# Residual product, norm and split of a two-block transformer: from separate stages to one stage each

## The reference, cut to what matters

```python
# block 1
x = x + g_a * (concat(y_m, y_a) @ w_out)                       # "mix"
x = x + g_f * conv_glu(modulate(rmsnorm(x, norm_ffn), sh_f, sc_f), w_up, conv, w_down)   # "down1"
x = rmsnorm(x, final_norm)                                     # "final1"
# block 2
h = rmsnorm_2(x, attn_norm_g)                                  # "norm2"
x = x + merge(mixers(h)) @ w_out_2                             # "out2"
h = rmsnorm_2(x, ffn_norm_g)
x = x + (silu(a) * b) @ w_down_2                               # "down2"; a, b = split(h @ w_up_2)
out = rmsnorm_2(x, final_norm_g)                               # "final2"
```

## Time and profile before

| | |
|---|---|
| median of 3 runs | 4328.44 us (4320.7 to 4330.6) |
| the profiled execution | 4323.73 us, span 4321.8 us |
| PE busy | 3732.9 us, 86% of the span |
| DVE busy | 1472.4 us, 34% |
| ACT busy | 1071.1 us, 25% |
| POOL busy | 812.3 us, 19% |
| mean granted TensorE clock | 0.924 |

### The profile page before, as it was taken

The page is one execution under the profiler, slowest core; times in us unless marked ns, Lnnn a source line. Parts: engine busy times, 40 slices in busy tenths (PEclk is TensorE's granted clock), DMA queues, the critical chain, the costliest instruction groups (busy, mean ns, idle before and its releaser), DMA issues. The chain is left out here.

```text
span 4321.8 us, 48005 instructions
## 1 busy us (share of the span) xinstructions
PE 3732.9 (86%) x17607; PEld 2966.1 (69%) x17607; DVE 1472.4 (34%) x2062; ACT 1071.1 (25%) x1871; POOL 812.3 (19%) x648
## 2 busy tenths in 40 slices
PE   5689799975999979946999895699998869999896
PEld 3467677863888867634888674377776648888674
DVE  5245352533333333342224443033343320000334
ACT  3423421223111122320222351033332220000222
POOL 3111132200333300012222453011111013332000
PEclk7799999987999989978999996799999979999998
DMA  7510111032111122112111014222222321111321
GB/s 233 191 26 23 40 32 58 1 110 75 49 49 49 39 102 88 63 68 47 44 49 60 29 28 106 56 91 92 90 91 99 104 68 49 49 49 29 131 91 69
DMA packets 282857, 304.16 MB, mean 70 GB/s; under 512 B 28810, under 2 KB 234794, under 8 KB 281046
## 3 DMA queue, kind: packets, MB, share of 16 engines
q1 hardware_dynamic: 279496, 275.57, 20.9%
q10 hardware_dynamic: 2846, 26.03, 1.9%
q0 software_dynamic: 384, 0.81, 0.1%
HBM read 261.03 MB, written 40.67 MB: 70 GB/s over the span
## 5 line engine op out<-in xcount | busy, mean ns | idle before, releaser
L170 PE MATMUL ps<-h_hi,w_hi 128*128 128x512 f32 x1408 | 549.7, 390 | 83.5 <-POOLq L200 83.5
L170 PE MATMUL ps<-h_lo,w_hi 128*128 128x512 f32 x1408 | 549.2, 390 | 0.0
L170 PE MATMUL ps<-h_hi,w_lo 128*128 128x512 f32 x1408 | 549.0, 390 | 0.0
L170 PEld LDWEIGHTS ps<-h_hi,w_hi 128*128 128x128 f32 x1408 | 265.4, 188 | 140.0 <-POOLq L200 85.1
L2187 PE MATMUL ps<-xn_hi,w_hi 128*128 128x512 f32 x608 | 250.1, 411 | 87.8 <-POOL w_lo L2152 49.7
L1600 PE MATMUL ps<-src_hi,w_hi 128*128 128x512 f32 x960 | 254.0, 404 | 81.8 <-ACTq L1555 75.7
L170 PEld LDWEIGHTS ps<-h_lo,w_hi 128*128 128x128 f32 x1408 | 265.4, 188 | 55.3
L170 PEld LDWEIGHTS ps<-h_hi,w_lo 128*128 128x128 f32 x1408 | 265.2, 188 | 55.1
L1571 DVE TENSOR_TENSOR w_lo<-w_raw,w_hi 128x1024 fp32r<-128x1024 f32 x120 | 147.0, 1225 | 443.6 <-ACTq L1555 443.5
L1600 PEld LDWEIGHTS ps<-src_hi,w_hi 128*128 128x128 f32 x960 | 185.0, 193 | 131.5 <-ACTq L1555 77.4
L198 POOL CAST w_hi<-xT 128x1024 fp32r<-128x1024 f32 x88 | 91.5, 1040 | 972.0 <-POOLq L61 622.8
(11 more groups left out here) (469 smaller groups left out, 6221.2 us busy)
## 6 DMA issues: line engine op xcount, KB each, us to landing
xT<-in_w_up SPq DMA_DIRECT2D x88, 512.0 KB, 4.9
w_raw<-in_w_down SPq DMA_DIRECT2D x88, 512.0 KB, 3.5
mg_raw<-in_w_gate SPq DMA_DIRECT2D x128, 256.0 KB, 2.6
wa<-in_w_ada SPq DMA_DIRECT2D x24, 1024.0 KB, 7.9
raw<-in_w_in SPq DMA_DIRECT2D x76, 256.0 KB, 2.9
w_raw<-in_w_out SPq DMA_DIRECT2D x32, 512.0 KB, 3.5
mg_raw<-in_w_branch SPq DMA_DIRECT2D x56, 256.0 KB, 2.6
xT<-x_saved ACTq DMA_DIRECT2D x3, 4096.0 KB, 13.6
```

The lines of the kernel that those rows point to most:

```text
L170: last = nc.tensor.matmul(bank_of(s, part, n)[:, 0:size], w[:, k, :], r[:, k, at:at + size], start=(k == 0 and j == 0), stop=(k == k_tiles ...
```

## The change

One function, `product_norm`, replaces `wide_product`, `residual`, `norm` and `split` in all four places. Within a single block it

- issues the load of the saved x first on SP, then the slabs; the slabs keep two raw slots, but the split slabs and sources have a ring of 5
- unrolls the steps (no hardware loops)
- after the first half's sums, lets PE go on with the second half's first four steps for 7 banks only (6 where two norms follow), and does the one or two banks left out ("late") for those four steps afterwards. In the late banks PE meanwhile puts the sum over partitions of the first half's squares, which POOL has added up over the 8 tiles
- has ACT form the inverse root as exp(-0.5·ln(mean + eps)), with no DVE reciprocal
- has DVE and ACT scale, round and make rests of the first half's tiles between the splits of the later steps of the second half
- for the second half does the same after the product, with PE summing the 8 squared tiles directly
- makes the two norms after down1 from one set of squares: a second sum, of squares weighted by the first gain's square, is formed by DVE (`weigh`) and gives the second inverse root; both scalings are done tile by tile (`scale`, `outer_scale`)
- saves x to DRAM per half, 2 MB each, once that half is final, and waits for both at the end of the block.

`end_stage` is now called at five more places: before each of the four fused stages, and after down1's.

The diff, cut to its core:

```diff
-def norm(c, name, parts, ones, out, shift=True, save=None):
-def split(c, x, hi, lo, name):
-def wide_product(...), def residual(...), def copy_wide(...)
+def product_norm(c, name, w, k_tiles, src, x, gate, first, bufs, h, gain, shift=None, outer=None, save=None, other=None):
+    K, R, DEFER = k_tiles, 5, 4
+    late = [DK - 1] if outer is None else [DK - 2, DK - 1]
...
+        @block.sync
+            sp.dma_start(first[0][:, :, :], first[1]).then_inc(first_loaded, 16)
+            for u in range(2 * K):
+                if u >= 2:
+                    sp.wait_ge(lo_made, u - 1)
+                sp.dma_start(raw[:, u % 2, :], w[:, u % K, :]).then_inc(loaded[u % 2], 16)
+            for half in saves:
+                x_ready(sp, half)
+                sp.dma_start(save[1][:, :, part(half)], save[0][:, :, part(half)]).then_inc(saved, 16)
+            if saves:
+                sp.wait_ge(saved, 32)
...
+        @block.scalar      # split_hi(u) waits loaded, and used >= u - R + 1
+            for u in range(K + R - 1):
+                split_hi(u)
+            square(0)
+            inverse(0)
+            for u in range(K + R - 1, 2 * K):
+                split_hi(u)
+                for _ in range(2 if K == DK else 1):
+                    if u > K + R and todo:
+                        rounding(0, todo.pop(0))
...
+            square(1)
+            inverse(1)
+            if h is not None:
+                for k in range(DK):
+                    rounding(1, k)
...
+        @block.vector
+            def take(half):
+                for m in range(DK):
+                    ... # x = x + gate * bank m, then_inc(taken, 1)
+                    if outer is not None and m:
+                        weigh(half, m - 1)
+            def tiles(half):
+                for k in range(DK + 1):
+                    if k < DK:
+                        scale(half, k)
+                    if k and h is not None and (half == 0 or k % 2 or outer is None):
+                        rest(half, k - 1)
+                    if k and outer is not None:
+                        outer_scale(half, k - 1)
+                    yield
+            for u in range(K + R - 1):
+                split_lo(u)
+            take(0)
...
+            take(1)
+            inverse(1)
+            for _ in tiles(1):
+                pass
+        @block.gpsimd
+            for k in range(1, DK):
+                pool.wait_ge(squared, k + 1)
+                step(nc.gpsimd.tensor_tensor(total(0), sq(0, 0) if k == 1 else total(0), sq(0, k), ALU.add))
+            if h is not None and outer is not None:
+                for k in range(1, DK, 2):
+                    ... # rest of tile k of the second half
+        @block.tensor
+            for u in range(K):
+                products(u, everything, True)
+            pe.wait_ge(used, K)
+            pe.nop().then_inc(summed, 1)
+            for u in range(K, K + DEFER - 1):
+                products(u, early, False)
+            pe.wait_ge(taken, DK)
+            pe.wait_ge(added, 1)
+            ... # one or two products with ones, into the late banks
+            products(K + DEFER - 1, early, False)
+            pe.wait_ge(mean_read, 1 if outer is None else 3)
+            for u in range(K, K + DEFER):
+                products(u, late, True)
+            for u in range(K + DEFER, 2 * K):
+                products(u, everything, True)
+            ... # second half: a product with ones per squared tile
```

More of the change, by code:

```diff
@@ L31 @@
 STREAM_AT = 204288
+HID_AT = 52416
+H_AT = HID_AT + 4 * FF * T // P
 HALVES = [(0, BANK), (BANK, BANK)]
@@ new lines, in _ @@
+            inverse(0)
+            todo = list(range(DK)) if h is not None else []
+            for u in range(K + R - 1, 2 * K):
[3 more added lines that the diff above has]
+                        rounding(0, todo.pop(0))
+            for k in todo:
+                rounding(0, k)
+            square(1)
+            inverse(1)
+            if h is not None:
+                for k in range(DK):
+                    rounding(1, k)
@@ L1616, in residual @@
[L1616 to L1635 removed]
+            step = c.dve.on(dve)
@@ new lines, in weigh @@
+            def weigh(half, k):
+                dve.wait_ge(squared, DK * half + k + 1)
+                if k == 0:
+                    ins = nc.vector.tensor_scalar(weighted(half), sq(half, 0), gain[:, 0, 0:1], None, ALU.mult)
+                else:
+                    ins = nc.vector.scalar_tensor_tensor(weighted(half), sq(half, k), gain[:, 0, k:k + 1], weighted(half), ALU.mult, ALU.add)
+                step(ins)
+                if k == DK - 1:
+                    dve.nop().then_inc(squares_weighed, 1)
@@ new lines, in inverse @@
+            def inverse(half):
+                if outer is None:
+                    dve.wait_ge(r_ready, half + 1)
+                    return
+                dve.wait_ge(mean_ready, half + 1)
+                dve.wait_ge(mean_read, 3 * half + 2)
+                nc.vector.tensor_tensor(root(half), c.ps[:, late[0] if half == 0 else 1, :], root(half), ALU.mult).then_inc(mean_read, 1)
+                dve.wait_ge(r_ready, 2 * half + 2)
+                step(nc.vector.tensor_tensor(r12(half), r12(half), r1(half), ALU.mult))
@@ new lines, in _ @@
+            for u in range(K + R - 1):
+                split_lo(u)
+            take(0)
+            if outer is not None:
+                inverse(0)
+            split_lo(K + R - 1)
+            work = tiles(0)
+            for u in range(K + R, 2 * K):
+                split_lo(u)
+                if u == K + R and outer is None:
+                    inverse(0)
+                for _ in range(2 if K == DK else 1):
+                    next(work, None)
+            for _ in work:
+                pass
@@ L2057, in turn_out @@
+    c.end_stage()
+    product_norm(c, "down2", io["w_down_2"][0], FK, hid, xT, None, (xT, saved[2]), product_buffers(c, "down2", H_AT), None,
+                 lambda k: gains[:, 5, k:k + 1], other=range(16, 21))
 def turn_out(c, io, xT, ident):
```

361 lines of the change are left out of this document (189 added, 172 removed).

## The result

The changed kernel takes 4197.5 us (median of 4 runs, 4196.9 to 4200.5) against 4329.5 for the kernel before (median of 4): 0.970 of its time, 95% interval 0.969 to 0.972. The forecast was 4209.5 with a range of 4188 to 4240. The profiled executions have spans of 4321.8 and 4195.6 us, 126.2 apart; the forecast had 119 for this pair.

A forecast was written before the change was run, and what follows sets the result against it. The prediction took PE's idle stretches, where engines work one after another around each norm, as the time to win. Stage savings of 29.7, 35.8, 30.2 and 23.3 took 4323.7 to 4204.7, median 4209.5, range 4188 to 4240.

The forecast's parts named there:

- The forecast case: Four fused stages together save 119 us, giving a median of 4209.5 us; chance 0.77.
- The tails: Norm work left after each product: ends at D+21.8 in mix, D+21.0 in out2, D+16.1 in down2, D+42.6 in down1.
- D: DVE's first bank read after a product's second half, the moment from which the prediction counts each tail.
- The sums: PE's eight sums of squares in the second half's tail: 7.8 us, with one slow one.
- The root: Inverse root in the tail: Ln and Exp 1.4 us, bounds 1.2 to 2.6; down1's chain of two roots 4.4 us.
- POOL: In down1, DVE and POOL hold each other up: +2.8 us at the half boundary, +3 in the last tiles.
- Half boundary: Added between a product's halves: +0.6 us in mix, out2 and down2, +7.7 in down1.
- End_stage: Each added end_stage call costs 0.75 us, at five places.
- The order: Loading x ahead of the slabs on SP's queue makes the first slab 1.5 us later per stage.
- Dry ring: Late ACT, POOL or root stalls PE in each second half and drops its clock: 44 us, giving 4254; chance 0.12.
- Spill: First half's tiles unfinished at product's end in the two 8-step stages, 12 us: 4222; slack 5 us; chance 0.07.
- Straight code: Unrolled products feed PE at only 0.30 us per matmul, not 0.227: 210 us, median 4420; chance 0.03.

The follow-up runs named there:

- e3_adds_late: Changed kernel with POOL's additions of down1's first-half squares starting only after DVE's eight weighings; 4194.6 us (1 run), stages 900.8 us.
- The second execution: The changed kernel executed again without any edit; 4198.3 us, four stages 904.6 us.
- e6_no_end_stage: Changed kernel without five end_stage calls: before mix, before and after down1, before down2, after out2; 4197.7 us (1 run), stages 901.0 us.
- e9_reciprocal: Changed kernel with Sqrt on ACT and reciprocal on DVE instead of Ln and Exp in mix, out2 and down2; 4202.8 us (1 run), stages 910.4 us.
- e4_x_behind: Changed kernel with the residual's load cut into eight 512 KB tiles and put behind the first slabs; 4158.6 us (4 runs), stages 863.5 us.
- e2_rests_dve: Changed kernel with down1's four POOL subtractions beside the last tiles given to DVE; 4204.0 us (1 run), stages 901.5 us.

## Why the prediction was right

**The forecast case held, and its terms were somewhat too dear.** The engines, waits and order of the work were those of the prediction; what differs is the size of some terms. The tails (D to the next product) gained 33.7, 47.8, 34.7 and 26.7, 142.9, where the terms gave 32.6, 45.8, 33.1 and 26.1, 137.5. What was added cost 10.5 (6.4 ahead of the first products, 4.1 in the products) instead of 9.0 + 9.5 = 18.5. 142.9 − 10.5 = 132.4.

**Tails.** The last tile's end was forecast at D+21.8 in mix and D+21.0 in out2, and came at D+21.3 and D+20.6. Down1's block was to end at D+42.6, and the next stage's first instruction came at D+42.6. That it agrees to the decimal is luck: DVE's last tile came at D+34.5 instead of D+35.1, and the save took 8.1 instead of 7.5. The sums took 7.1 us and not 7.8: no slow one, for PE's gap of 1.7 us left the clock at 1.00. The root took the two ACT instructions (0.69 and 0.63) that were guessed from rows, and the chain of two roots 4.3 us (1804.12 to 1808.45) against 4.4. The upper bound of 2.6 for Ln and Exp "if each needs a table load" was reckoned too low (two loads of 1.28 on top of 1.4 make 4.0), but no load came.

**POOL.** The rule that speaks against the edit was right in down1's tail: four tiles longer by 1.0 each, 4.0 against the 3 taken. In the half boundary it was mis-sized. The prediction charged PE with 2.8 us for six banks at a pace of 2.0 us. The reads came 1.7 to 2.05 us apart and only from the third on, since POOL's first addition begins 2.2 us after the first read: the sixth bank was 1.1 us late, and the 2.8 are what all eight reads and weighings lost together (`e3_adds_late`). That is 1.7 of the 3.4 us by which down1's product grew less than forecast (4.3 and not 7.7); the other half is not accounted for.

**Half boundary.** +0.6 was forecast for the other three; measured −3.1, +2.4 and +0.5. The clock decides the first two. In the four microseconds that begin 4 us after the first bank read it was granted so, in mix before and after, in out2 before and after:

```profile
946.96:950.96 4.00, 4.00 (x9) 2.69 (x9) 3.18 (x5) 0.00 (x0) 0.00 (x0) 0.50 0.00 0
957.54:961.54 4.00, 3.75 (x15) 2.90 (x16) 1.36 (x3) 1.95 (x4) 3.77 (x4) 1.00 0.00 0
3406.10:3410.10 4.00, 3.80 (x15) 2.73 (x15) 2.70 (x4) 0.00 (x0) 0.00 (x0) 1.00 0.02 6
3339.02:3343.02 4.00, 4.00 (x13) 3.00 (x14) 0.88 (x2) 1.54 (x3) 3.77 (x4) 0.69 0.00 0
```

In mix it fell before and not after, in out2 the other way round. The second execution, in which it fell in mix too, has mix's product at 96.0, −0.7 beside 96.7 before. Terms of half a microsecond are smaller than what the clock does at this place. In mix and down2 it is chance: from first to last matmul the product of down2 took 245.4 to 245.9 us in three executions where it stayed at 1.00 (`e3_adds_late`, `e6_no_end_stage`, `e9_reciprocal`) and 247.1 to 247.2 in the six where it fell. In out2 it fell in both executions of the changed kernel and in every experiment, and not in the one trace of the kernel before, so that those 2.4 us may be a cost of the change. One trace of before can't decide it.

**End_stage and the load's order.** The 0.75 was too dear: `e6_no_end_stage` bounds it at about half a microsecond and can't tell it from nothing. At the end of mix and out2, from the last rest to the next product, it took 10.8 and 10.9 us with the call there and 10.6 and 11.4 without. The order was taken at 1.5 us a stage: from first issue to first cast 14.3, 13.9, 13.6 and 13.4 us instead of 12.2, 12.7, 12.2 and 13.3, 1.2 on the mean. The size was right and the question too small. I noted that the slab "already paid for sharing" with the 4 MB and asked only what the new order adds; what the sharing cost was 10 us in each stage of the changed kernel (`e4_x_behind`). In the kernel before it was not tried; by the 3.2 to 4.4 us of a slab that goes first, its 12.2 to 13.3 hold some 9 us of the same, an estimate.

**The rivals.** Dry ring: no gap before the fifth to eighth step, and additions late by 8 us still didn't empty it. The slack was reckoned for the splits and taken for POOL's too, whose sum is not needed until 6 us after the additions end (965.2 and 971.35 in mix). Spill: the first half's tiles ended at 996.2 in mix, 5.6 us ahead of D, as reckoned (5). Straight code: full steps of 24 matmuls take 5.44 us as in the earlier trace rows; PE is fed without its loops.

**The whole time.** The median lies 12.0 us under the forecast. 13.3 are the stages' terms; chance outside the stages takes 6.1 of that back; and 4.7 were added to carry the profiled time over to a median, while the profiled execution of the changed kernel was its median. So the distance that the whole time shows is partly luck; the gain of the stages was 132 for 119, a tenth off. The range's upper end is not the sum of its terms (24 + 8 + 7 + 5 = 44, not 26), but none of the four came. A single execution of this program can't be forecast to a few microseconds, since the time up to the first stage alone moves by 20.

## What to carry to other kernels

When a product, a norm and a split are put in one stage, reckon the barriers, passes and roots that go apart from the work that is hidden: here the first gave 82 us and the second 48.5. Before moving a load, ask what it shares its landing time with, not only what it stands behind: a big transfer that isn't needed until half a stage later belongs in pieces behind the first small one. Give an idle engine work only after looking at which port it shares: four subtractions on POOL lengthened DVE's by 4.0 us to save 2.7.

## What the runs showed of the hardware

- The granted clock of identical code differs between executions: 0.91 to 0.94 over the same 300 us, and the first 880 us of the program end anywhere between 872 and 893. Single executions of two kernels can't be compared to 10 us in whole; cut at matching instructions they can, to about 1 us where the clock didn't differ and to 2 or 3 where it fell in one and not in the other (mix 144.0 and 147.0 us in the two executions of the changed kernel).
- A POOL subtraction and a DVE instruction that both read two SBUF tiles stretch each other, 0.74 to 1.75 us and about 1.27 to 1.66 (`e2_rests_dve` against the changed kernel); a DVE instruction with a PSUM input is not touched (0.75).
- A slab of 512 KB is being rounded 3.2 to 4.4 us after its issue when it goes out first (`e4_x_behind`), and 13.0 to 14.2 after its own issue when 4 MB are issued just before it.
